# Two small row stores moved ahead of a 2 MB weight load on the load queue, in a two-layer diffusion block

## The reference, cut to what matters

```python
mod = jnp.split((silu_c @ ada_w[l] + ada_b[l])[:, None, :], 6, axis=-1)
...
h = modulate(rms_norm(x, mix_pre_g[l]), mod[0], mod[1])
y, yc = even_mixer(h, hc, even_w_in[e], even_w_out[e], ...)
x = x + mod[2] * rms_norm(y, mix_post_g[l])
h = modulate(rms_norm(x, ffn_pre_g[l]), mod[3], mod[4])
x = x + mod[5] * rms_norm(conv_ffn(h, ffn_w_in[l], ffn_conv_w[l], ffn_w_out[l]), ffn_post_g[l])
```

## Time and profile before

| | |
|---|---|
| median of three executions | 1707.03 us (1700.58 to 1708.42) |
| profiled execution, its own time | 1700.58 us |
| its span, first to last instruction | 1698.8 us |
| TensorE busy | 1610.8 us, 95% of the span |
| VectorE busy | 1023.7 us, 60% |
| ScalarE busy | 554.9 us, 33% |
| mean granted TensorE clock | 0.986 of full speed |
| DMA | 169.43 MB, mean 100 GB/s |

### The profile page before, as it was taken

How to read it: one execution, slowest core, us unless ns; L and a number is a source line. 1 busy time by engine, 2 the same in 40 slices (tenths; PEclk the granted TensorE clock), 3 DMA queues, 4 the chain that set the end, 5 groups by cost and what they waited for, 6 DMA issues and landing times.

```text
span 1698.8 us, 21966 instructions
## 1 busy us (share of the span) xinstructions
PE 1610.8 (95%) x8698; PEld 1346.8 (79%) x8698; DVE 1023.7 (60%) x1448; ACT 554.9 (33%) x883; POOL 54.7 (3%) x74
## 2 busy tenths in 40 slices
PE   6999999877999999999999999899999999999998
PEld 2688887666888887888888887787778888888886
DVE  2899995755657676466634435754884644344344
ACT  2313215472443231032211223632333543232133
POOL 0500000110000000000000001100000000000001
PEclk9999999988999999999999999999999999999999
DMA  9421221304314543444424222130001233233222
GB/s 304 137 64 56 69 74 44 125 31 91 109 51 149 197 174 124 149 149 165 157 80 144 65 85 63 66 124 25 26 1 50 86 100 113 74 99 112 85 90 85
DMA packets 134009, 169.43 MB, mean 100 GB/s; under 512 B 15970, under 2 KB 92450, under 8 KB 133930
## 3 DMA queue, kind: packets, MB, share of 16 engines
q1 hardware_dynamic: 133360, 168.11, 30.9%
q10 hardware_dynamic: 570, 0.22, 0.1%
HBM read 166.17 MB, written 2.15 MB: 99 GB/s over the span
## 4 chain that ended last, share of the span: by engine, by line
PE 75%; DVE 15%; ACT 4%; issue 2%; POOL 1%; POOLq 0%; DVEq 0%; ACTq 0%
PE acc L671 39%; PE acc L725 21%; DVE conv_u L1775 6%; PE acc L697 3%; DVE w_lo L1507 2%; PE acc L876 2%; PE acc L1072 2%; PE acc L1051 2%; PE acc L777 1%; PE acc L1019 1%; PE acc L642 1%; PE acc L911 1%; DVE x L1674 1%; DVE y L1507 1%; POOL y L2156 1%
## 5 line engine op out<-in xcount | busy, mean ns | idle before, releaser
L671 PE MATMUL acc<-h_hi,w_hi 128*128 128x512 f32 (+1 forms) x1424 | 415.8, 353 | 7.4 <-DVE w_lo L1507 4.4
L671 PE MATMUL acc<-h_hi,w_lo 128*128 128x512 f32 (+1 forms) x1424 | 411.5, 350 | 0.0
L671 PE MATMUL acc<-h_lo,w_hi 128*128 128x512 f32 (+1 forms) x1424 | 411.5, 350 | 0.0
L1507 DVE TENSOR_TENSOR w_lo<-raw,w_hi 128x1024 fp32r<-128x1024 f32 x186 | 222.8, 1228 | 155.2 <-ACT w_hi L1090 155.2
L1090 ACT ACTIVATE w_hi<-raw 128x1024 fp32r<-128x1024 f32 x186 | 189.1, 1055 | 246.9 <-PE acc L725 211.1
L671 PEld LDWEIGHTS acc<-h_hi,w_hi 128*128 128x128 f32 x1424 | 229.9, 188 | 45.4 <-DVE w_lo L1507 4.8
L671 PEld LDWEIGHTS acc<-h_lo,w_hi 128*128 128x128 f32 x1424 | 229.9, 188 | 38.5 <-issue 0.5
L671 PEld LDWEIGHTS acc<-h_hi,w_lo 128*128 128x128 f32 x1424 | 229.2, 188 | 37.9
L725 PE MATMUL acc<-w_hi,hid_hi 128*128 128x512 f32 x440 | 175.8, 400 | 0.0
L725 PE MATMUL acc<-w_lo,hid_hi 128*128 128x512 f32 x440 | 175.1, 398 | 0.0
L725 PE MATMUL acc<-w_hi,hid_lo 128*128 128x512 f32 x440 | 174.9, 398 | 0.0
(11 more groups left out here) (234 smaller groups left out, 2027.8 us busy)
## 6 DMA issues: line engine op xcount, KB each, us to landing
ada_w<-in_ada_w SPq DMA_DIRECT2D x88, 512.0 KB, 6.0
raw<-in_ffn_w_in SPq DMA_DIRECT2D x88, 512.0 KB, 3.7
raw<-in_ffn_w_out SPq DMA_DIRECT2D x44, 512.0 KB, 4.4
raw<-in_even_w_in SPq DMA_DIRECT2D x24, 512.0 KB, 4.6
ada<-in_ada_w SPq DMA_DIRECT2D x8, 1024.0 KB, 12.2
raw<-in_odd_w_in SPq DMA_DIRECT2D x12, 512.0 KB, 4.3
raw<-in_even_w_out SPq DMA_DIRECT2D x8, 512.0 KB, 4.7
ada_m<-in_ada_w SPq DMA_DIRECT2D x8, 512.0 KB, 3.8
```

What stands on the lines that cost most here:

```text
L671: last = nc.tensor.matmul(acc[:, s, m, t0:t1], w[:, slot, kk, c], x_[:, k, t0:t1], start=(k == 0 and q == 0), stop=(k == KD - 1 and q == 2))
L1507: return nc.vector.tensor_tensor(out_, in0, in1, op)
```

## The change

The two stores of the gate rows are issued ahead of chunk c0 instead of behind it. Nothing else differs: the same DMAs, waits and instructions are there, and `load_beside` takes c0 together with c1 and k6.

```diff
             sp.wait_ge(gates_set, 1)
-            load_beside("out0", w_even_out, 0, (("c", 0),))
             gate_rows(0, 0, 2, 2)
-            load_beside("out0", w_even_out, 0, (("c", 1), ("k", 6)))
+            load_beside("out0", w_even_out, 0, (("c", 0), ("c", 1), ("k", 6)))
             sp.wait_ge(gates_out, 32)
             gates_everywhere(0, gates[0], 2)
             load_beside("out0", w_even_out, 0, (("k", 7),))
```

## The result

The changed kernel takes 1717.19 us (median of five; 1715.59 to 1719.53), 10.2 us above the median of 1707.03 before. The ratio of the two kernels, for which 23 executions of the changed one are on record, is 1.0075, with a 95% interval from 1.0058 to 1.0091: 12.8 us slower on 1707.03. The profiled execution has a span of 1717.0 us.

A forecast was written before the change was run, and what follows sets the result against it. TensorE, busy 95% of the span, was taken to bound the kernel; 6.3 us of wait plus 1.75 of clock gave 8.1 us, 1715 us against the median of 1707.03 (ratio 1.0047), range 1706 to 1720.

The forecast's parts named there:

- within 0.5%: Case that the change in time stays within 0.5% (8.5 us), not told from no change; chance 0.59.
- Rival A: Empty queue doesn't shorten the stores' 16.9 us; TensorE waits 11.3 us, up to 1722 us; milder form 1719; chance 0.20.
- Cover of c0: VectorE ends c0's sums at 422.20, TensorE's small products begin at 422.54: 0.34 us, the thinnest cover in the stage.
- Step 2: Stores issued first hold the DMA queue from 405.7 for 10.5 us, over at 416.2 (415.0 to 417.3).
- Steps 3 and 4: c0's part 0 lands at 418.2 instead of 408.3; VectorE's sums take 10.64 us without idle time, ending at 428.9.
- Step 5: TensorE, at c0's small products at 422.54, waits until 428.9: 6.3 us (5.1 to 7.4).
- Step 6: After TensorE's wait the granted clock is 0.50 for a stretch, losing 1.75 us (bounds nothing and 3.5).
- Step 7: c1's sums on VectorE move with c0's; their 4.9 us cover before TensorE wants them stays.
- Step 8: Gate rows land at 416.2 instead of 423.1, but their load moves to about 430; the gain is nothing.
- Rival B: Stores on an empty queue are short, over by 409.9; TensorE doesn't wait, time stays 1707; chance 0.12.
- Rival C: Other executions of the old kernel already wait 3.4 us for c0; change adds 4.7 us or less, 1711 to 1712; chance 0.19.
- Rival D: Faster by over 0.5%, through a change in timing of later stages that can't be named; chance 0.04.

## Why the prediction was right and wrong

The mechanism was right at every step, and both large terms were sized too low: 6.3 us for c0's delay against 8.5, and 1.75 for the clock against 4.3, together 8.1 against 12.8. The measured ratio's interval begins at 1.0058, above the forecast of 1.0047 and above the 0.5% line, so the likeliest case, "within 0.5%", was the wrong one. The time of 1717.19 lies in the range, 2 us from the 1715 given, but by the ratio the miss is 4.7 us, and 1.0075 on 1707.03 would be 1719.8, just below the range's end of 1720. That the range held owes more to its width, taken from Rival A, than to the sum.

- *Cover of c0, 0.34 us.* Right, and the key: putting the columns 8.3 us later brought 12.8 down to 2.7.
- *Step 2, the hold.* Forecast from 10.7 to 13.0 us after the first issue, taken as 11.9. Measured 13.5, beyond the upper bound by 0.5. I had let the empty queue shorten the time of the first pair. I had also counted the start of the movement from the row's start at 404.50 and not from the issue at 404.29, which is 0.2 us. The additional stores show that most of the hold is there already with the smallest of them: 9.0 us for 128 elements, 10.8 for 1024, 13.5 for 2048, 20.5 for 4096, each from the first issue.
- *Steps 3 and 4.* Part 0 landed 2.5 us after the stores (forecast 2.0), and the sums took 423.27 to 434.00, 10.73 us (10.64), without an idle stretch inside.
- *Step 5, the wait.* 7.75 us against 6.3. c0's sums ended 26.7 us after the release against 24.6 in the forecast, 2.1 later; TensorE's own first products, longer at half clock, hid 0.75 of that.
- *Step 6, the clock.* The term that failed most: 1.75 taken, 4.3 measured (1.73 in the small products, 2.55 in the large ones), above the bound of 3.5. The granted clock was still 0.50 for 8.9 us after TensorE went on. My precedents had large products behind the gap, or a gap after which the small products still ran at 1.00 (647.8 to 650.3 us, just ahead of the half-clock row); here 3.6 us of one-column products stood first, and after those the large products still ran at half speed for 5.3 us. The filled wait showed the term by itself, 4.4 us. The five other kernels with a wait at c0's columns, of 4.4 to 15.3 us, took 3.57 or 3.58 us for the small products and 18.1 to 18.9 for the 72 large ones, 3.4 to 4.2 us more than before: the term hardly goes by the length of the wait.
- *Step 7.* Right. c1's sums ended at 448.4 and TensorE wanted them at 456.66.
- *Step 8.* Right: nothing was gained. The gate rows landed earlier by the stage's clock (13.5 against 18.9 us after the release), but the gates' load went out at 435.58.
- *Rival A* in its milder form (stores over 14.2 us after the release, two stretches of clock, 12.1 us) came nearest. *Rival B* holds only for stores of another form: 1.4 us for runs of 32 or 64 bytes or for elements apart. There the roughly 2 us that the Trainium skill's "DMA: Bandwidth & Descriptors" (anatomy of one DMA, a section on DMAs issued from GpSimd, unlike these) gives as the fixed cost of a DMA is near what is measured; for neighbouring 4-byte elements the measured 9.0 to 20.5 us decide. *Rival C* fell: two kernels in which nothing holds c0 gave 0.9991 and 1.0000; its 3.4 us would be 0.9980, at the edge of the first interval (from 0.9979) and outside the second (from 0.9988), and the change cost 12.8 us, not 4.7. *Rival D* didn't occur.

What stays open is why neighbouring 4-byte writes wait. Spacing alone turned 9.0 us into 1.4, so it isn't the number, bytes or size of writes by themselves; that writes from different DMA engines meet in one place of DRAM fits it, but this is not shown: no view tells which engine writes which element, and no run varied it. The run apart also used one row of DRAM more than the run side by side. The packets of the two real stores are recorded some 11 us before the landing. As far as such records tell, the time isn't spent on working the packets off; they don't say where it is spent.

## What to carry to other kernels

Before moving a small DMA ahead of a load, look up its landing time in the trace, not its size: here 8 KB held all the loads behind it for 13.5 us, on its own queue and on another. Then ask how much cover the load has; 0.34 us can't hide anything, and a product moved 8 us later could. When a new wait of TensorE is priced, add the half-clock products behind it: 3.4 to 4.4 us here, where short ones came first. And where a small store lands late, try its form before its place: as 8 runs of 512 bytes the same rows held nothing.

## What the runs showed of the hardware that was not expected

- 128 writes of 4 bytes, side by side in DRAM, landed after 9.0 us; the same 128 set 64 bytes apart after 1.4 us, and 128 runs of 32 or 64 bytes side by side after 1.4 us.
- While such writes are open, loads behind them move at 4 to 24 GB/s instead of 343. Loads of another engine's queue are caught too: 14.8 us for 512 KB, while 51 GB/s moved from 412 to 418 us.
- The records of 2048 such writes end about 2.5 us after the first issue, and the stores land 13.5 us after it.
- After 7.75 us without work the granted clock stayed at 0.50 for 8.9 us: 3.6 us of one-column products and 5.3 us of large ones. With the gap filled it stayed at 1.00.
